# An MoE encoder block: four late expert tiles instead of two, and the expert rows loaded ahead of the last down weights

## The chip, the cores and the metric

One core of a Trainium2 chip runs the kernel. The time is the device time of one execution, in microseconds (us). Engines are named PE (TensorE), DVE (VectorE), ACT (ScalarE), POOL (GpSimd) and SP (SyncE, which here only issues transfers).

## What is computed

A two-part block on x of 512 rows by 1024 columns, all in float32. The first part (a gated causal convolution beside a sparse attention, merged and projected) is not touched by the change. The second part and the end are:

```python
h = rms_norm(x, g_ffn)
# top-1 group of 4, then top-2 of the 8 experts in it; comb = their softmax weights
for e in range(32):                       # D_MODEL 1024, EXPERT_FF 256
    a, b = h @ w_gate[e], h @ w_up[e]
    out += (silu(a) * b * comb[:, e]) @ w_down[e]
x = x + out
return rms_norm(x, g_final)
```

Each of the 512 rows goes to two experts, so there are 1024 (row, choice) products to make. The weights of an expert are 3 MB, those of all 32 are 96 MB.

## The kernel before, in words

`build` writes one program for each engine, with waits on semaphores between them. In the expert part the 32 experts are worked on in 16 pairs. A tile is 32 slots of each of the two experts of a pair; a pair has as many tiles as its fuller expert needs. The number of tiles is known only at run time: a table `tab` on the chip holds for each pair where its tiles start, and each engine loops over registers read from it. With the inputs here there are 30 tiles, 0 to 29. The pairs are put in an order by their size; the last pair (15) has one tile, tile 29, and pair 14 has tiles 27 and 28.

**Weights.** Three slots of on-chip memory (region 0, region 1, and `gates` with `conv_buf`) take turns. For pair n SP waits until the pair three before it has let go of each part, and issues eight copies of 0.5 MB for gate and up (`load_half`, L429) and two copies of 1 MB for down (`load_down`, L439). All go through SP's queue and are spread over 16 DMA engines. In `pair_tiles` (L1003) PE waits for them: `ld_gu` at L1012, `ld_dn` at L1034.

**One tile** (`pair_tiles`). 64 small products of gate and up (L1022) into bank 0; the transposes of the next tile's rows (`transpose_tile`, L980, L985) into banks 6 and 7; ACT takes the silu (L1376), DVE multiplies (L1803), PE transposes the result (L1031), DVE copies it (L1806); then 16 down products (L1039) into bank 2. ACT copies bank 2 to the buffer `ys` (L1383). POOL gathers the input rows of later tiles from memory (L622) and scatters the results to the table of expert rows in memory (L665, `expert_rows`), one half row per slot.

**The late tiles.** The last two tiles, 28 and 29, are not scattered: their entries of the scatter's index are set out of bounds (L1781), their places in `expert_rows` are set to zero by two scatters of zeros (L635), and their results are kept on the chip in the stack `late`, 128 slots by 1024. A weighted one-hot matrix `col_w` (rows by slots, made by DVE at L1784 to L1787, before tile 0) is transposed by PE (L1052) into `place`, and eight products (`late_rows`, L1076) bring the stack into the right rows, 128x512 each.

**The end.** After the last weights SP loads `g_final` (L486), waits until the scatters of tiles 0 to 27 have landed (L489), and loads the expert rows back, eight copies of 0.5 MB, one for each block b of 128 rows and each choice c (L493). For c=0, and for block 3's c=1, DVE adds the weighted rows (`add_row`, L1815); for the other c=1 rows PE makes weighted products (`weighted_row`, L1068) into the banks where `late_rows` adds its own. DVE adds each bank to x (`add_late`, L1823), ACT takes the squares (L1397), DVE the mean (L1415), POOL the power -1/2 (L671), DVE scales (`scale_out`, L1829), and SP stores (L497, L502).

The order of all this is written out by hand; each engine's program is in order. What sets the order of the transfers is SP's program:

```python
                sp.wait_ge(S["y_mm"], used)
                load_down(slot, pair)            # L482, the last of the weights
            ...
            for n in range(RING):
                sp.wait_ge(scattered[n], ((early + (RING - 1 - n)) // RING) * 16)
            sp.wait_ge(zeroed, 32)
            for b in range(TB):                  # L491
                for c in range(2):
                    sp.dma_start(y_row(b, c), ...)
```

`early` is the number of tiles that are scattered, 28 here.

Of the kernel before, what the change touches and what calls it, by code (L numbers as in the profile page):

```python
# [21 lines left out]
I32 = mybir.dt.int32  # L22
U32 = mybir.dt.uint32
# [43 lines left out]
def build(nc, x, g_mix, w_in, conv_w, conv_b, conv_ln_g, conv_ln_b, w_conv_out, w_attn_out, w_out,  # L67
# [17 lines left out]
    MAXT = 48  # L85
    assert PAIRS + (2 * T - PAIRS) // SLOTS < MAXT
# [13 lines left out]
    with ExitStack() as ctx:  # L100
# [116 lines left out]
        def piece(words):  # L217
# [32 lines left out]
        place = gluf[:, cut[0] - 256:cut[0] + 256]  # L250
        no_rows = gluf[:, 0:BANK]
        diag = gluf[:, BANK:BANK + 3 * P].rearrange("p (b n) -> p b n", b=TB - 1)
        col_code = mask[:, P:2 * P]
        col_hit = gluf[:, BANK:2 * BANK].rearrange("p (b n) -> p b n", b=TB)
        col_w = mask[:, 2 * P:6 * P].rearrange("p (b n) -> p b n", b=TB)
        first_hit = kTf[:, BANK:BANK + 2 * TB * SLOTS].rearrange("p (b e n) -> p b e n", b=TB, e=2)
        late = r1[:, 8192 + D:8192 + 2 * D].rearrange("p (n f) -> p n f", n=2)
        late_si = sb("late_si", [P, 2], U32)
# [5 lines left out]
        gidx = sb("gidx", [P, MAXT + RING + 1], U32)  # L264
        carrier = sb("carrier", [P, 6])
# [33 lines left out]
            hidT_mm hidT_ev y_mm yev_a xg_mm xtev_a xtev_v idx_copy y_add hits_ready first_mm diagw_ready late_ev col_ready late_ready place_mm place_ev late_mm late_add o_ready dve_chain pool_chain  # L299
# [66 lines left out]
        late_banks = (3, 4, 0, 1, 5, 6, 7, 2)  # L366
# [9 lines left out]
        def _(sp):  # L376
# [94 lines left out]
            sp.wait_ge(S["order_ready"], 1)  # L471
            for n in range(SETS, PAIRS):
# [11 lines left out]
            early = sp.value_load(tab[0:1, PAIRS + 1:PAIRS + 2], min_val=PAIRS - 2, max_val=MAXT - 3)  # L484
            sp.wait_ge(S["y_mm"], sp.value_load(tab[0:1, PAIRS - 2:PAIRS - 1], min_val=1, max_val=MAXT))
            sp.dma_start(g_final_bc, g_final.rearrange("(a n) -> a n", a=1).to_broadcast([P, D])).then_inc(ld_gbc, 16)  # L486
            for n in range(RING):

                sp.wait_ge(scattered[n], ((early + (RING - 1 - n)) // RING) * 16)  # L489
            sp.wait_ge(zeroed, 32)  # L490
            for b in range(TB):  # L491
                for c in range(2):
                    sp.dma_start(y_row(b, c), y_dram[c * T + b * P:c * T + (b + 1) * P, :])\  # L493
                        .then_inc(ld_y[b][c], 16)
# [3 lines left out]
            for n in range(RING):  # L498
                sp.wait_ge(scattered[n], ((early + 2 + (RING - 1 - n)) // RING) * 16)
# [1385 lines left out]
```

## Time and profile before

| | |
|---|---|
| time, median of 3 executions | 661.61 us (659.83 to 662.32) |
| the profiled execution's own time | 662.68 us |
| its span | 660.6 us |
| mean granted clock of PE | 0.966 of full |
| PE busy | 581.6 us, 88% |
| DVE, ACT, POOL busy | 345.2, 257.1, 294.8 us |
| read from memory, written | 145.11 MB, 12.60 MB |
| SP's copies (queue q1) | 139.90 MB, 57.0% of 16 engines' span |

The span is from the first to the last instruction; the execution's own time is 2.1 us longer. The expert loop starts at 390.75 us, the last down product ends at 633.4. A busy share over the whole span says little here, as stages with different limits follow on each other. "PEclk" is the clock that PE was granted: 1.0 is 2.4 GHz and 0.5 is 1.2 GHz. "SPq" is SP's queue: the time that it takes to issue transfers.

### The profile page before, as it was taken

The numbers are of one execution on the slowest core, as the hardware profiler recorded it, in microseconds if no ns is written. First come the engines' busy times: TensorE is split into PE (matmuls) and PEld (weight loads), VectorE is DVE, ScalarE is ACT, GpSimd is POOL, SyncE is SP. The second block draws the span as 40 slices with busy tenths as digits, with TensorE's granted clock in tenths as the row PEclk, the third lists the DMA queues.
The fourth block names the chain that finished last, engine by engine and source line by source line (L and its number), as shares of the span: only waits on it lengthen the run. The fifth ranks groups of instructions, "written<-read, shape, count | busy, mean of one in ns | idle before, by whom it ended". The sixth has DMA issues, their size and how long they took to land.

```text
span 660.6 us, 12497 instructions
## 1 busy us (share of the span) xinstructions
PE 581.6 (88%) x4387; PEld 384.8 (58%) x4388; DVE 345.2 (52%) x855; ACT 257.1 (39%) x444; POOL 294.8 (45%) x466
## 2 busy tenths in 40 slices
PE   3899999999999999999999876973899899988883
PEld 2577788877665676877888632432444444444431
DVE  4518999999979996169322583110111211211156
ACT  6435333244755674364413103331133333334212
POOL 5333344469996322346550016443245445544331
PEclk9999999999999999799999796998899999999987
DMA  9122632622222024031249999999997999999863
GB/s 296 46 88 65 224 95 66 137 63 65 64 65 64 0 89 168 0 128 52 108 168 357 376 406 350 408 406 408 409 405 292 409 410 407 409 406 402 350 242 127
DMA packets 64609, 149.09 MB, mean 226 GB/s; under 512 B 14372, under 2 KB 30756, under 8 KB 64574
## 3 DMA queue, kind: packets, MB, share of 16 engines
q1 hardware_dynamic: 59150, 139.90, 57.0%
q0 software_dynamic: 5280, 8.22, 3.4%
q10 hardware_dynamic: 144, 0.52, 0.2%
q8 instruction: 20, 0.33, 0.2%
q14 instruction: 15, 0.12, 0.1%
HBM read 145.11 MB, written 12.60 MB: 239 GB/s over the span
## 4 chain that ended last, share of the span: by engine, by line
PE 51%; DVE 21%; SPq 11%; DMA 9%; issue 4%; ACT 3%; POOL 1%; DVEq 0%; POOLq 0%; ACTq 0%
PE bank L704 27%; SPq L429 8%; PE bank L1022 7%; PE bank L1039 5%; DVE bm L1477 5%; DVE m L1476 4%; DMA conv_buf<-in_w_e_down 3%; DMA region<-in_w_e_up 3%; DVE conv_buf L1468 3%; SPq L439 2%; PE bank L782 2%; DMA region<-expert_rows 2%; PE bank L815 2%; PE bank L803 1%; PE bank L985 1%
## 5 line engine op out<-in xcount | busy, mean ns | idle before, releaser
L704 PE MATMUL bank<-h_hi,w_part 128*128 128x512 f32 (+1 forms) x528 | 173.4, 398 | 3.2 <-DVE h_lo L1426 1.7
L557 POOL TENSOR_TENSOR w_part<-region,w_part 128x1024 fp32r<-128x1024 f32 (+1 forms) x52 | 109.8, 2112 | 147.6 <-ACT w_part L1113 147.6
L704 PEld LDWEIGHTS bank<-h_hi,w_part 128*128 128x128 f32 (+1 forms) x528 | 98.0, 186 | 30.3 <-issue 6.8
L704 PE MATMUL bank<-h_lo,w_part 128*128 128x512 f32 (+1 forms) x264 | 102.9, 390 | 0.0
L1803 DVE TENSOR_TENSOR mask_b<-mask_b,bank 128x128 f32<-128x128 f32 x30 | 8.7, 289 | 176.8 <-ACT mask_b L1376 176.8
L1022 PE MATMUL bank<-region,kT 128*32 128x256 f32 x1408 | 82.5, 387 | 14.4 <-DMA region<-in_w_e_up 11.5
L1113 ACT ACTIVATE w_part<-region 128x1024 fp32r<-128x1024 f32 (+1 forms) x52 | 48.0, 925 | 108.0 <-PE bank L704 107.9
L607 POOL TENSOR_TENSOR carrier<-mhalf 128x1 f32<-128x1 f32 x183 | 33.3, 199 | 115.2 <-ACT qT L1383 97.5
L1022 PEld LDWEIGHTS bank<-region,kT 128*32 128x32 f32 x1408 | 50.3, 112 | 53.0 <-issue 31.4
L1511 DVE SCALAR_TENSOR_TENSOR bank<-glu,cv,bank 128x256 f32<-128x256 f32 x196 | 78.6, 479 | 0.0
L704 PEld LDWEIGHTS bank<-h_lo,w_part 128*128 128x128 f32 (+1 forms) x264 | 49.1, 186 | 9.6
L1039 PE MATMUL bank<-region,mask_b 128*32 128x512 f32 x352 | 44.0, 619 | 9.9 <-DVE mask_b L1806 9.9
L1383 ACT ACTIVATE qT<-bank 128x512 f32 x28 | 16.7, 597 | 80.6 <-PE bank L1039 80.6
L622 POOL DMA_INDIRECT bm<-h_rows,gi x34 | 36.5, 1074 | 5.0 <-issue 0.2
L665 POOL DMA_INDIRECT expert_rows<-qT,si x30 | 30.7, 1023 | 13.2 <-issue 13.1
L1376 ACT ACT_TABLE_LOAD x28 | 35.9, 1283 | 0.5
L1376 ACT ACTIVATE mask_b<-bank 128x128 f32<-128x128 f32 x30 | 8.3, 278 | 67.0 <-PE bank L1022 67.0
L1022 PE MATMUL bank<-gates,kT 128*32 128x256 f32 x512 | 29.2, 380 | 5.6 <-DMA gates<-in_w_e_up 5.1
L985 PE MATMUL bank<-ident,v_rows 128*128 128x128 f32 x124 | 23.5, 313 | 7.6 <-DVE v_rows L1798 6.8
L1022 PEld LDWEIGHTS bank<-gates,kT 128*32 128x32 f32 x512 | 18.4, 110 | 19.3 <-issue 11.8
L985 PEld LDWEIGHTS bank<-ident,v_rows 128*128 128x128 f32 x124 | 17.4, 209 | 20.9 <-issue 13.6
L565 POOL TENSOR_SCALAR bm<-glu,cv 128x512 f32<-128x512 f32 x17 | 26.6, 1565 | 0.9
(289 smaller groups left out, 909.3 us busy)
## 6 DMA issues: line engine op xcount, KB each, us to landing
region<-in_w_e_down SPq DMA_DIRECT2D x22, 1024.0 KB, 15.9
region<-in_w_e_gate SPq DMA_DIRECT2D x44, 512.0 KB
region<-in_w_e_up SPq DMA_DIRECT2D x44, 512.0 KB
region<-in_w_in SPq DMA_DIRECT2D x16, 1024.0 KB, 6.1
conv_buf<-in_w_e_down SPq DMA_DIRECT2D x10, 1024.0 KB, 18.5
gates<-in_w_e_gate SPq DMA_DIRECT2D x20, 512.0 KB
gates<-in_w_e_up SPq DMA_DIRECT2D x20, 512.0 KB
region<-in_w_out SPq DMA_DIRECT2D x2, 2048.0 KB, 7.8
```

The source lines that it names most:

```text
L429: sp.dma_start(w_gu[slot][:, e, m, half, :, :], w[0, bass.ds(pair * 2 + e, 1), rows, :].rearrange("a (p k) f -> p (a k) f", k=KD // 2))\
L557: g.tensor_tensor(unit_part(u, 1), unit_raw(u), unit_part(u, 0).bitcast(F32), ALU.subtract)\
L607: ins = g.tensor_tensor(carrier[:, n:n + 1], mhalf[:], mhalf[:], ALU.add)
L622: g.indirect_dma_start(out=ring[:, u, :], out_offset=None, in_=h2_halves, in_offset=bass.IndirectOffsetOnAxis(ap=gi1[:, u:u + 1], axis=0), ...
L704: last = mm(out_, a_parts[p], b_parts[q], start=start and x_ == 0, stop=stop and x_ == 2)
L985: last = tr(bank[6 + k // 2][:, k % 2 * P:(k % 2 + 1) * P], view[:, k, :], ident[:])
L1022: last = mm(bank[0][32 * c:32 * c + 32, 0:FF], xTs[:, k, at_:at_ + 32], w_gu[slot][:, e, :, half, k, j * P:(j + 1) * P], start=(half == 0 ...
L1039: last = mm(bank[2][32 * c:32 * c + 32, :], hidT[:, at_:at_ + 32], w_dn[slot][:, e, j, n * BANK:(n + 1) * BANK], start=(j == 0), stop=(j = ...
L1113: a(unit_part(u, 0), unit_raw(u), ACT.Copy).then_inc(S["w_hi"], 1)
L1376: a(sil, bank[0][:, 0:P], ACT.Silu).then_inc(S["silu_g"], 1)
L1477: link(v.match_replace(work[:, 0:n], m8[:], src[:, 0:n], NEG))
L1511: ins = v.scalar_tensor_tensor(out_, shifted, cv[:, c, j:j + 1], so_far, ALU.mult, ALU.add)
```

## The change

The constant `LATE = 4` takes the place of the two late tiles: tiles 26 to 29 are held back, as two stacks of two tiles, `late[0]` (26, 27) and `late[1]` (28, 29), with two `col_w` and two `place`. Four scatters of zeros stand ahead of the loop instead of two. SP issues the copies of the expert rows (`load_rows`) inside the loop over pairs, for the last pair, after its gate and up weights and before its down weights; they wait only for tiles 0 to 25. DVE makes `col_w` after tile 3 and after tile 5 instead of before tile 0. PE transposes the placements before pair 12. The eight products of stack 0 are made inside tile 29: three before its gate products, three before its hidden copy is waited for, one before its down products, one among the products of stack 1, which follow on the down products. Of the rows with c=1 only block 3's are weighted by PE, all others are added by DVE, three of them ahead of the last tile's hidden product and four behind it. ACT copies both halves of each late tile (before, DVE took one half of tile 29), and takes the squares of block 3 in two halves. If the last pair had more than one tile, the products would be made in each of them (`again`); here it is zero.

```diff
+    LATE = 4
-        late_banks = (3, 4, 0, 1, 5, 6, 7, 2)
+        late_banks = (3, 4, 5, 6, 7, 0, 1, 2)
@@ SP
+            def load_rows():
+                sp.wait_ge(S["y_mm"], sp.value_load(tab[0:1, PAIRS - 2:PAIRS - 1], min_val=1, max_val=MAXT))
+                for n in range(RING):
+                    sp.wait_ge(scattered[n], ((early + (RING - 1 - n)) // RING) * 16)
+                sp.wait_ge(zeroed, 16 * LATE)
+                for b in range(TB):
+                    for c in range(2):
+                        sp.dma_start(y_row(b, c), y_dram[c * T + b * P:c * T + (b + 1) * P, :])\
+                            .then_inc(ld_y[b][c], 16)
...
                 load_half(slot, pair, 1)
+                if n == PAIRS - 1:
+                    load_rows()
                 sp.wait_ge(S["y_mm"], used)
                 load_down(slot, pair)
-            sp.wait_ge(S["y_mm"], sp.value_load(tab[0:1, PAIRS - 2:PAIRS - 1], min_val=1, max_val=MAXT))
             sp.dma_start(g_final_bc, ...).then_inc(ld_gbc, 16)
-            for n in range(RING):
-                sp.wait_ge(scattered[n], ((early + (RING - 1 - n)) // RING) * 16)
-            sp.wait_ge(zeroed, 32)
-            for b in range(TB):
...
@@ POOL
-            for u in range(2):
+            for u in range(LATE):
                 g.indirect_dma_start(out=y_halves, ...)
@@ PE, pair_tiles
                 with pe.Fori(first, end) as t:
+                    if last_pair:
+                        pe.wait_ge(S["place_ev"], 2)
+                        pe.wait_ge(S["yev_a"], pe.value_load(rows_upto[0:1, bass.ds(t, 1)], min_val=1, max_val=MAXT))
+                        for k in range(3):
+                            late_rows(0, k)
                     pe.wait_ge(ld_gu[slot], 128 * turn + 128)
...
                     tr(bank[1][:, 0:P], hid, ident[:]).then_inc(S["hidT_mm"], 1)
+                    if last_pair:
+                        pe.wait_ge(S["xtev_a"], t + 2)
+                        pe.wait_ge(S["xtev_v"], t + 2)
+                        for k in range(3, 6):
+                            late_rows(0, k)
                     pe.wait_ge(S["hidT_ev"], t + 2)
                     pe.wait_ge(S["yev_a"], t + 1)
+                    if last_pair:
+                        late_rows(0, 6)
                     pe.wait_ge(ld_dn[slot], 32 * turn + 32)
...
                     last.then_inc(S["y_mm"], 1)
+                    if last_pair:
+                        pe.wait_ge(S["diagw_ready"], 1)
+                        pe.wait_ge(ld_y[TB - 1][1], 16)
+                        weighted_half(0)
+                        half_done = pe.value_load(half_upto[0:1, bass.ds(t, 1)], min_val=1, max_val=LATE)
+                        for k in range(2 * TB):
+                            if k == 0:
+                                pe.wait_ge(S["late_half"], half_done)
+                            elif k == 1:
+                                pe.wait_ge(S["yev_a"], t + 2)
+                            late_rows(1, k)
+                            if k == 3:
+                                late_rows(0, 2 * TB - 1)
+                                weighted_half(1)
@@ ACT
-            for u in range(2):
+            for u in range(LATE):
+                if u < 2:
+                    act.wait_ge(S["place_mm"], u + 1)
+                    a(place[u], bank[5 - u][:], ACT.Copy).then_inc(S["place_ev"], 1)
                 hidden_gate(early + u)
-                for n in range(2 - u):
+                for n in range(2):
                     for e in range(2):
...
+                    if n == 0:
+                        last.then_inc(S["late_half"], 1)
@@ DVE
-            with dve.Fori(0, early + 1) as t:
+            for t in range(6):
+                next_rows(t)
+                hidden(t)
+                if t in (3, 5):
+                    late_columns((t - 3) // 2)
+            with dve.Fori(6, early + LATE - 1) as t:
                 next_rows(t)
                 hidden(t)
...
+            rows_in = [(b, c) for b in range(TB) for c in range(2)][:-1]
+            next_rows(early + LATE - 1)
+            for b, c in rows_in[0:3]:
+                add_row(b, c)
+            hidden(early + LATE - 1)
+            for b, c in rows_in[3:]:
+                add_row(b, c)
+            for k in range(4):
+                add_late(k)
             mean_square(2, 0)
+            add_late(4)
             dve.wait_ge(ld_gbc, 32)
             scale_out(0, whole)
+            add_late(5)
             mean_square(2, 1)
+            add_late(6)
+            add_late(7)
             scale_out(1, whole)
             mean_square(2, 2)
             scale_out(2, whole)
```

## Rows read from the trace of the kernel before

**Rows 1.** The page: mean busy share of the DMA engines in 40 equal slices, tenths.

```profile
DMA  9122632622222024031249999999997999999863
```

**Rows 2.** Chain of waits in order of time, from 540 us: start, us, what.

```profile
618.53 6.08 DMA expert_rows<-qT,si
...
625.01 10.21 DMA region<-expert_rows
```

**Rows 3.** Timeline of SP's queue: start, us of issuing, engine, line, operation, tiles, count.

```profile
610.68 4.07 SPq L439 DMA_DIRECT2D region<-in_w_e_down  x2
...
624.63 3.74 SPq L493 DMA_DIRECT2D region<-expert_rows  x8
```

**Rows 4.** L439's and L493's transfers: down copies issued from 610 to 616; row copies.

```profile
L439 SPq DMA_DIRECT2D region<-in_w_e_down x2: 1506/1988/2471, 610.7 to 612.3; - x2
...
DMA to landing us min/median/max: 11.4/15.2/19.0
...
DMA to landing us min/median/max: 9.3/12.2/14.8
```

**Rows 5.** Windows of 2 us: length, PE, PEld, DVE, ACT, POOL busy, PEclk, DMA share, GB/s.

```profile
624.00:626.00 2.00, 0.41 (x4) 0.17 (x2) 0.00 (x0) 1.97 (x4) 0.00 (x0) 1.00 0.55 182
...
636.00:638.00 2.00, 2.00 (x4) 0.83 (x3) 1.91 (x2) 0.00 (x0) 0.48 (x1) 0.50 0.48 187
638.00:640.00 2.00, 2.00 (x4) 0.76 (x3) 0.03 (x1) 0.00 (x0) 0.00 (x0) 0.67 0.18 68
640.00:642.00 2.00, 2.00 (x6) 0.91 (x5) 1.90 (x3) 0.52 (x1) 0.00 (x0) 1.00 0.06 25
```

**Rows 6.** Timeline of PE: down product of tile 0; placement; last tile.

```profile
403.59 3.64 PE L1039 MATMUL bank<-region,mask_b 128*32 128x512 f32 x16 [0.38 <-DVE mask_b L1806]
...
623.75 0.66 PE L1052 MATMUL bank<-ident,mask 128*128 128x128 f32 x4
626.40 3.66 PE L1022 MATMUL bank<-region,kT 128*32 128x256 f32 x64 [1.99 <-DMA region<-in_w_e_up]
631.49 1.92 PE L1039 MATMUL bank<-region,mask_b 128*32 128x512 f32 x16 [0.38 <-DVE mask_b L1806]
```

**Rows 7.** Windows of 4 us around PE's long wait for weights, columns as in rows 5.

```profile
460.00:464.00 4.00, 0.00 (x0) 0.00 (x0) 0.00 (x0) 0.00 (x0) 0.00 (x0) 0.50 1.03 409
464.00:468.00 4.00, 3.71 (x36) 2.03 (x40) 0.00 (x0) 0.00 (x0) 0.00 (x0) 0.50 1.03 410
```

**Rows 8.** Timeline of the end, all engines.

```profile
623.88 2.39 ACT L1393 ACTIVATE region<-bank 32x512 f32<-32x512 f32 x4 [2.64 <-PE bank L1039]
...
633.91 1.28 DVE L1815 SCALAR_TENSOR_TENSOR x_rows<-region,wts,x_rows 128x1024 f32<-128x1024 f32 x1 [2.48 <-DMA region<-expert_rows]
...
640.56 1.88 PE L1068 MATMUL bank<-region,glu 128*128 128x512 f32 x4
...
642.28 1.88 PE L1076 MATMUL bank<-region,glu 128*128 128x512 f32 x4
...
650.89 1.28 DVE L1823 TENSOR_TENSOR x_rows<-x_rows,bank 128x512 f32<-128x512 f32 x2
...
652.21 1.06 ACT L1397 ACTIVATE conv_buf<-x_rows 128x1024 f32<-128x1024 f32 x1 [1.24 <-DVE x_rows L1823]
...
654.32 0.54 POOL L671 TENSOR_TENSOR rs<-ss,mhalf 128x1 f32<-128x1 f32 x1 [1.46 <-DVE ss L1415]
...
654.90 1.41 DVE L1829 SCALAR_TENSOR_TENSOR x_rows<-x_rows,rs,region 128x512 f32<-128x512 f32 x2 [0.66 <-POOL rs L671]
```

**Rows 9.** Timeline of the start of the expert loop.

```profile
399.05 0.69 DVE L1787 TENSOR_TENSOR mask<-mask,glu 128x512 f32<-128x512 f32 x1
...
400.73 0.45 DVE L1798 COPY v_rows<-bm 128x512 f32 x1 [0.99 <-POOL carrier L607]
...
402.73 0.48 PE L1031 MATMUL bank<-ident,mask_b 128*128 128x128 f32 x1 [0.36 <-DVE mask_b L1803]
...
404.17 1.03 POOL L635 DMA_INDIRECT expert_rows<-glu,late_si  x1 [0.16 <-issue]
```

More of the change, by code:

```diff
@@ L498, in _ @@
             for n in range(RING):
[L499 removed]
+                sp.wait_ge(scattered[n], ((early + LATE + (RING - 1 - n)) // RING) * 16)
             for n in range(2):
@@ L1001, in table_products, with late_rows, weighted_half, pair_tiles @@
                 last.then_inc(S["tab_mm"], 1)
-            def pair_tiles(n, slot, turn):
+            def late_rows(stack, k):
+                b, n = late_turns[k]
+                last = mm(bank[late_banks[k]][:], place[stack][:, b * P:(b + 1) * P], late[stack][:, n, :],
+                          start=(stack == 0), stop=(stack == 1))
+                if stack:
+                    last.then_inc(S["late_mm"], 1)
+            def weighted_half(n):
+                mm(bank[late_banks[2 * TB - 2 + n]][:], diag, y_row(TB - 1, 1)[:, n * BANK:(n + 1) * BANK],
+                   start=False, stop=False)
+            def pair_tiles(n, slot, turn, last_pair=False):
                 first = pe.value_load(tab[0:1, n:n + 1] if isinstance(n, int) else tab[0:1, bass.ds(n, 1)],
@@ L1046, in _ @@
                 pair_tiles(slot, slot, 0)
[L1047 removed]
+            with pe.Fori(1, PAIRS // SETS - 1) as i:
                 for slot in range(SETS):
                     pair_tiles(SETS * i + slot, slot, i)
[L1050 to L1088 removed]
+            pe.wait_ge(S["col_ready"], 2)
+            for stack in range(2):
+                for b in range(TB):
+                    last = tr(bank[5 - stack][:, b * P:(b + 1) * P], col_w[stack][:, b, :], ident[:])
+                last.then_inc(S["place_mm"], 1)
+            early = pe.value_load(tab[0:1, PAIRS + 1:PAIRS + 2], min_val=PAIRS - LATE, max_val=MAXT - 1 - LATE)
+            for n in range((PAIRS // SETS - 1) * SETS, PAIRS):
+                pair_tiles(n, n % SETS, n // SETS, n == PAIRS - 1)
         @block.scalar
@@ L1366, in _ @@
             act.wait_ge(S["tab_ready"], 1)
-            early = act.value_load(tab[0:1, PAIRS + 1:PAIRS + 2], min_val=PAIRS - 2, max_val=MAXT - 3)
-            act.wait_ge(S["col_ready"], 1)
-            for b in range(TB - 1):
-                last = a(diag[:, b, :], ident[:], ACT.Copy, scale=wts[:, 1, b:b + 1])
-            last.then_inc(S["diagw_ready"], 1)
+            early = act.value_load(tab[0:1, PAIRS + 1:PAIRS + 2], min_val=PAIRS - LATE, max_val=MAXT - 1 - LATE)
             def hidden_gate(t):
```

133 lines of the change are left out of this document (49 added, 84 removed).

## The prediction

> **What bounds the kernel now.** I read the page's slices first: the DMA engines are full in nearly every slice of the last 40% of the span [rows 1]. Then the chain of waits in order of time: before the end it passes through a scatter's landing (6.08 us) and the landing of the expert rows (10.21 us) [rows 2]. The queue of SyncE shows the order behind that: the last pair's down weights are issued at 610.68, the eight row copies only at 624.63, when the scatter of tile 27 has landed [rows 3]. The landings tell how deep the queue is: the second down copy, issued at 612.3, lands 19.0 us later, at 631.3; the last row copy, issued at 627.9 (the eighth of eight within 3.74 us), lands 14.8 us later, at 642.7 [rows 4]. The two-microsecond windows show that the engines don't end together. At 624 to 626 their mean share is 0.55 and at 636 to 638 it is 0.48, but the last data come after 640, at a share of 0.06, which is one engine of 16 [rows 5]. So one engine is some 5 us behind the bulk of them, and a copy has landed only when that one has done its part. That late engine sees no hole at 624 to 626: down weights until 631.3, then the final gain (0.5 MB), then eight rows of 0.5 MB until 642.7, which is (642.7 - 631.3) / 9 = 1.27 us for 0.5 MB, its full pace.
>
> PE meanwhile starts tile 29 (the last; its pair has only this one) at 626.40, held by its gate and up weights, and its down product at 631.49, ends at 633.41 [rows 6]. From there to the end of the span, 660.6, are 27.2 us: row adds, late rows, norm, store.
>
> **The change part by part.**
>
> *1. Rows ahead of the last down weights.* The eight row copies now stand in SyncE's queue before the two down copies. On an engine the queue is served in order in every row here, so the down weights land 8 x 1.27 = 10.2 us later on the late engine: 631.3 + 10.2 = 641.5. The bulk of the engines finish the rows at about 637 now (share 0.48 in 636 to 638 [rows 5]); without the hole (some 1.8 us) and with the final gain behind instead of ahead (1.3) they would be through with everything at about 634. I take the late engine, since PE waits for all 16; the bulk value is the other bound. The Trainium skill (DMA: Bandwidth & Descriptors, "Queues, rings and completion order") says that each engine consumes its descriptors in ring order and that a copy is complete only when all of its engines have finished; this speaks against the change, and the landing rows agree.
>
> SyncE's new waits in front of the rows are for tile 26's down product, the scatters up to tile 25 and the zeroing. Behind them stand the down copies and the final gain; PE waits for the first. Tile 26 ends before tile 27's product begins and SyncE comes to this point at 610.68 [rows 3], so I cost the waits at 0 to 1 us, take 0, and the cover is the queue's backlog of some 15 us. The hole in the bulk's work (0.45 of 2 us in 624 to 626, and a similar one before) is filled, but the late engine gains nothing from that. The final gain moves behind the down weights, 641.5 + 1.3 = 642.8, and is wanted only at the first scaling, after 650: nothing.
>
> *2. PE before the last down product.* Three first-stack products ahead of tile 29 cost 3 x 0.86 (two products lie 1.72 apart, from 640.56 to 642.28 [rows 8]) = 2.6 us. They fit between 624.4 and PE's old start at 626.40 but for about 0.6 to 1 us. Gate and up 3.66, transposes and hidden about 1.5, then four more products, 3.4: PE is ready at about 635.8. Against 641.5 all of this is free; against the bulk's landing it would be the bound. Placement is transposed for both stacks, eight instead of four at 0.66 us a group [rows 6], before pair 12 instead of after pair 14: 1.3 to 2.2 us with the issue gap. PE waits for DMA at tile 27 anyway, so at most 1 us comes through and is then covered by the late landing: 0.
>
> *3. The clock.* PE will stand idle from 635.8 to 641.5, over 5 us. When it stood idle up to 464 the granted clock was 0.50 at 460 to 464 and still 0.50 at 464 to 468 [rows 7]: 1.2 GHz. The down product at this level took 3.64 us at 403.59, against 1.92 at 631.49 [rows 6]. I take 3.64: the product ends at 641.5 + 0.1 + 3.64 = 645.2. The other bound is 1.92. The Trainium skill (TensorE: Matmul & The Clock Gate, "The HAM clock gate") calls the halved clock the default that activity lifts; with it the product costs 1.7 us more than a reading by the last tile of the trace, and rows 7 agree.
>
> *4. The tail behind that product.* Time counted from its end, E. ScalarE copies the first half of the stack: 2 x 0.60 (four took 2.39 [rows 8]), done at E+1.35. The second half is done at E+2.55. PE meanwhile makes one weighted half. Then come products 0 at E+1.4 and 1 at E+2.6, and to the end of product 3 it is E+5.2. The held-back first-stack product and the second weighted half take two more (E+6.9), products 4 to 7 four more: E+10.4. DVE adds each at 0.64 (two took 1.28). Add 4 starts at E+7.9. From there DVE is the bound: add 4 0.64, scaling 1.28, add 5 0.64, adds 6 and 7 1.28, scaling 1.28, small operations 0.25, then 0.75 waiting for POOL's power, scaling 1.28, two linked small operations 0.4, POOL 0.54 + 0.1, two half scalings 1.41: E+17.8. The squares of the last block are done in halves by ScalarE before E+13.2 (half of 1.06 each, an estimate), hidden. From DVE's last scaling (656.31) to the end are 4.3 us in the trace. Sum: 22.1 us, against 27.2 now, so 5.1 us are gained. What goes: five row adds of 1.28 and two products' worth of waiting for rows. I put this sum at 21 to 23.
>
> *5. The start.* Five column operations of 0.7 us (the last at 399.05) and ScalarE's wait for them leave the way to tile 0 [rows 9]. But DVE's row copy at 400.73 waits for the first gather, and stays; only ScalarE's late silu goes, and the transpose of the hidden rows can follow the row transposes at about 402.4 instead of 402.73. That is 0.35 us, carried on by the full DMA queue. The columns, 3.5 us, go into DVE's idle time in tiles 3 and 5, where a tile lasts 7 us and DVE waits over 5 of it: 0; with this cover gone it would be 3.5 each. Two more zeroing scatters on POOL, 1.03 and a gap each, some 2.6 us, delay tile 1's rows to about 410.3, just when PE wants them (tile 1's gate products end near 410.4): 0, at worst 0.5. Their bytes are saved again at the scatters of tiles 26 and 27, which now write nothing. ScalarE's four quarter copies (2.39 instead of 0.60) in tiles 26 and 27 end before PE's next down product: 0. Unrolled loops on PE and DVE: code is loaded in the shade of a PE that waits for DMA, 0; the trace doesn't show their cost, and I allow -0.5 to 1.5.
>
> **Sum.** 641.5 + 0.1 + 3.64 + 22.1 - 0.35 = 667.0 us of span against 660.6: +6.4. The profiled execution's own time was 662.68, 2.1 over its span and 1.1 over the median of 661.61. 661.6 + 6.4 = 668.0.
>
> **The rivals.** (A) *The lag of one engine does not show in the changed kernel*, or the down weights' last part doesn't suffer it. They land at about 634, PE's own 635.8 is the bound, the clock stays full: 635.9 + 1.92 + 22.1 - 0.35 = 659.6, one less than now, no measurable change (about 660.6 on the median). For it: the mean share at 638 to 640 is only 0.18 [rows 5], so most engines really are early. Against: the last landings of both groups of copies [rows 4], each waited for by the engine that came next. (B) *Faster*: the same early landing, and the late products fit into the tile. PE waits in each tile for the silu, the row copies and the hidden copy; if three of the seven hide there, the down product starts at 633.2 rather than 635.9 and the span is 656.9, on the median 657.9 (-0.6%). It decides at a landing of 636.8: a down product at full clock that starts later is no gain (636.8 + 0.1 + 1.92 + 22.1 - 0.35 = 660.6). (C) *Slower still*: the waits in front of the rows bite or late products run at half clock beyond the down product, 2 to 3 us on top: about 671.
>
> **How the numbers follow.** About 0.5% is what a measurement of this kernel can tell from no change, 3.3 us. My forecast has 0.62, C 0.12, A 0.17, B 0.09. For 8 in 10 the range runs from the lower edge of the forecast's case with part of A, 660.0, to 671.0. Faster 0.09; same 0.18 (A and the low edge of the forecast); slower 0.73.
>
> **What would show it.** In the changed profile: the rows' issues directly behind the last up weights, near 611, and the down copies near 620 to 624; the DMA share full through 636 with no hole at 624; the last down product near 641.6, with "DMA region<-in_w_e_down" as what ended PE's idle time, 5 us of it, and PEclk at 0.5; row adds done before it; 22 us from its end to the span's. I am wrong if the down product starts before 637, if its clock is full, or if the tail behind it is under 21 us.

## The result, and the profile after

| | before | after |
|---|---|---|
| time, median | 661.97 us (659.83 to 662.73, 4 executions) | 669.61 us (667.56 to 671.22, 4 executions) |
| span of the profiled execution | 660.6 us | 667.0 us |
| expert loop starts | 390.75 us | 391.69 us |
| PE busy | 581.6 us, 88% | 589.9 us, 88% |
| mean granted clock | 0.966 | 0.964 |

The change makes the kernel slower: the ratio is 1.0125, with a 95% interval of [1.01, 1.015], 7.6 us by the medians and 6.4 us by the profiled spans. The loop starts 0.9 us later in this execution. Over the seven profiled executions of kernels with the kernel before's tiles (before, e2, e5, e6, e9, e10, e12) its start lies between 389.0 and 391.4 us, 390.3 in the mean; over the seven with four late tiles (after, e1, e3, e4, e7, e8, e11) between 390.8 and 392.7, 391.8 in the mean. The two ranges overlap, and whether the 1.5 us between the means belong to the change is not shown. So below the span is also given from the loop's start (the first gate product): 269.9 us before, 275.3 after. What is lost ahead of the loop is not in it; it is in the ratios.

The page of after, the mean busy share of the DMA engines in 40 equal slices; it answers to [rows 1]:

```profile
DMA  9122722522222033033069999999998999999913
```

The queue of SyncE after, to be set beside [rows 3] (start, us of issuing, line, operation, tiles, count; L486 loads the rows, L443 the down weights, L502 the final gain):

```profile
610.59 1.16 SPq L433 DMA_DIRECT2D region<-in_w_e_up  x1
612.93 9.20 SPq L486 DMA_DIRECT2D region<-expert_rows  x8
622.24 3.45 SPq L443 DMA_DIRECT2D region<-in_w_e_down  x2
625.74 0.48 SPq L502 DMA_DIRECT2D region<-in_g_final  x1
```

The rows follow the last up weights after 1.2 us, so their new waits held SP for little. They take 9.20 us to issue where they took 3.74; it fits with this that in e2 below, whose queue had run nearly dry, they take 4.79, so I read the 9.20 as the pace of a full queue. The down weights leave 11.6 us later than before.

The chain of waits, in order of time, answers to [rows 2]. The scatter and the row copies are gone from it, and one piece stands in their place:

```profile
623.35 18.27 DMA region<-in_w_e_down
641.67 2.71 PE bank L1073 x16
```

The timeline of PE, for [rows 6] (L1015 is `late_rows`, two records to a product; L1049 gate and up, L1073 down, L1022 the weighted half rows):

```profile
625.92 2.84 PE L1015 MATMUL bank<-glu 128*128 128x512 f32 x6 [0.61 <-issue]
628.68 3.66 PE L1049 MATMUL bank<-region,kT 128*32 128x256 f32 x64
...
633.63 3.67 PE L1015 MATMUL bank<-glu 128*128 128x512 f32 x8 [0.18 <-issue]
641.67 2.69 PE L1073 MATMUL bank<-region,mask_b 128*32 128x512 f32 x16 [4.36 <-DMA region<-in_w_e_down]
644.28 2.02 PE L1022 MATMUL bank<-region,mask 128*128 128x512 f32 x2
646.13 3.60 PE L1015 MATMUL bank<-region,glu 128*128 128x512 f32 x8
```

Everything that could be done ahead of the last down product is done at 637.3, and PE then stands until 641.67. Before, the same product began at 631.49. The windows of 2 us (columns as in [rows 5]):

```profile
634.00:636.00 2.00, 2.00 (x6) 0.91 (x5) 1.97 (x2) 0.00 (x0) 1.01 (x1) 1.00 0.48 185
636.00:638.00 2.00, 1.30 (x4) 0.23 (x2) 1.93 (x3) 0.00 (x0) 0.00 (x0) 1.00 0.32 123
638.00:640.00 2.00, 0.00 (x0) 0.00 (x0) 0.93 (x1) 0.00 (x0) 0.00 (x0) 1.00 0.21 84
640.00:642.00 2.00, 0.33 (x4) 0.16 (x8) 0.00 (x0) 0.00 (x0) 0.00 (x0) 1.00 0.09 35
642.00:644.00 2.00, 2.00 (x16) 0.26 (x8) 0.00 (x0) 0.00 (x0) 0.00 (x0) 0.67 0.01 4
644.00:646.00 2.00, 2.00 (x6) 0.79 (x3) 0.00 (x0) 1.56 (x3) 0.00 (x0) 0.50 0.00 0
```

Two things are to be seen. The DMA share falls to 0.48 at 634 and to 0.09 at 640, though the down weights have landed only at 641.6, and PE waits for them from 637.3 on. A share of 0.09 is 1.4 engines of 16: a few engines carry the rest. And the clock is still 1.00 while PE stands; it falls only when the product has begun. The row adds, DVE's, all lie before the product, as intended (L1851; the first add of a bank, L1859, follows at 647.19):

```profile
627.72 3.97 DVE L1851 SCALAR_TENSOR_TENSOR x_rows<-region,wts,x_rows 128x1024 f32<-128x1024 f32 x3 [2.75 <-DMA region<-expert_rows]
...
633.69 5.24 DVE L1851 SCALAR_TENSOR_TENSOR x_rows<-region,wts,x_rows 128x1024 f32<-128x1024 f32 x4
```

From the product's end at 644.36 to the end of the span are 22.6 us, against 27.2 before. So the change buys 4.55 us at the end and pays for them with a product that ends 10.95 us later (644.36 against 633.41): 6.4 us more.

### The profile page after: what moved, and what is told of

The parts are those of the page before. It is cut to its first block, busy times and chain, and to the rows that moved or that the text cites. A ratio compares the mean times of both kernels' runs of the same rounds, so it can differ in the third digit from the quotient of the medians.

```text
span 667.0 us, 12502 instructions
## 1 busy us (share of the span) xinstructions
PE 589.9 (88%) x4395; PEld 387.2 (58%) x4400; DVE 350.1 (52%) x866; ACT 258.7 (39%) x451; POOL 299.8 (45%) x468
## 4 chain that ended last, share of the span: by engine, by line
PE 56%; DVE 17%; SPq 9%; DMA 7%; issue 5%; ACT 3%; POOL 1%; another core or an unknown queue 0%; POOLq 0%; DVEq 0%; ACTq 0%
PE bank L713 26%; PE bank L1049 10%; PE bank L1073 6%; SPq L433 6%; DVE bm L1499 5%; DVE m L1498 4%; DMA region<-in_w_e_down 3%; DVE conv_buf L1490 3%; PE bank L791 2%; DMA region<-in_w_e_up 2%; PE bank L994 2%; SPq L443 2%; PE bank L824 2%; PE bank L812 1%; SPq L486 1%
## 5 line engine op out<-in xcount | busy, mean ns | idle before, releaser
L1049 PE MATMUL bank<-region,kT 128*32 128x256 f32 x1408 | 83.4, 386 | 9.0 <-DMA region<-in_w_e_up 6.5
L616 POOL TENSOR_TENSOR carrier<-mhalf 128x1 f32<-128x1 f32 x183 | 34.9, 208 | 120.1 <-ACT qT L1396 89.7
L1049 PEld LDWEIGHTS bank<-region,kT 128*32 128x32 f32 x1408 | 50.2, 112 | 48.5 <-issue 26.6
L1073 PE MATMUL bank<-region,mask_b 128*32 128x512 f32 x352 | 44.8, 628 | 13.9 <-DVE mask_b L1837 8.7
L1049 PE MATMUL bank<-gates,kT 128*32 128x256 f32 x512 | 31.7, 403 | 6.8 <-DMA gates<-in_w_e_up 5.9
L1049 PEld LDWEIGHTS bank<-gates,kT 128*32 128x32 f32 x512 | 19.1, 116 | 22.3 <-issue 15.4
L994 PE MATMUL bank<-ident,v_rows 128*128 128x128 f32 x124 | 23.5, 313 | 6.2 <-DVE v_rows L1829 5.3
L1073 PEld LDWEIGHTS bank<-region,mask_b 128*32 128x32 f32 x352 | 9.6, 111 | 32.6 <-issue 24.2
```

Of the source, the lines that this page charges most:

```text
L616: ins = g.tensor_tensor(carrier[:, n:n + 1], mhalf[:], mhalf[:], ALU.add)
L994: last = tr(bank[6 + k // 2][:, k % 2 * P:(k % 2 + 1) * P], view[:, k, :], ident[:])
L1049: last = mm(bank[0][32 * c:32 * c + 32, 0:FF], xTs[:, k, at_:at_ + 32], w_gu[slot][:, e, :, half, k, j * P:(j + 1) * P], start=(half == 0 ...
L1073: last = mm(bank[2][32 * c:32 * c + 32, :], hidT[:, at_:at_ + 32], w_dn[slot][:, e, j, n * BANK:(n + 1) * BANK], start=(j == 0), stop=(j = ...
```

## The experiments

Twelve runs follow; e11 is the changed kernel again and e12 is e9 again. The figures of each, with the kernel before timed beside it on the same chip:

| kernel | ratio to before, 95% | span from the loop's start |
|---|---|---|
| before | | 269.9 |
| after | 1.0125 [1.01, 1.015] | 275.3 |
| e1, rows behind | 1.0135 [1.0084, 1.0186] | 276.7 |
| e2, order alone | 1.018 [1.0129, 1.0231] | 281.7 |
| e3, three ahead | 1.0038 [1.0014, 1.0062] | 273.0 |
| e4, kept busy | 1.0079 [1.0055, 1.0103] | 276.3 |
| e5, gain last | 0.9963 [0.9937, 0.999] | 267.4 |
| e6, ScalarE copies | 1.0 [0.9973, 1.0027] | 268.1 |
| e7, adds behind | 1.0054 [1.0022, 1.0086] | 272.4 |
| e8, last row late | 1.0017 [0.9987, 1.0047] | 270.0 |
| e9, gain before last row | 0.9982 [0.9956, 1.0008] | 266.7 |
| e10, last row on PE | 1.0009 [0.9986, 1.0031] | 267.9 |
| e11, after again | 1.0136 [1.0091, 1.0182] | 276.9 |
| e12, e9 again | 0.9961 [0.9941, 0.9981] | 267.8 |

The last column is of one profiled execution each; after and e11, or e9 and e12, are the same kernel and differ by 1.6 and 1.1 us in it. The profiled executions of e3 and e4 were moreover the slowest of their kernels, some 4 us above the medians (667.42 against 663.45, 670.72 against 666.45). So a difference of 2 us in this column is the least that says something by itself, and for e3 and e4 the ratio is the better figure.

### Is it the order of the transfers?

**e1, the changed kernel with the rows issued behind the down weights.**

```diff
-                if n == PAIRS - 1:
-                    load_rows()
                 sp.wait_ge(S["y_mm"], used)
                 load_down(slot, pair)
+                if n == PAIRS - 1:
+                    load_rows()
```

> The changed kernel with one edit: the eight row copies are issued behind the two last down copies again. Theory 1 (the copies of one DMA engine are served in order and the last engine decides, so the rows ahead cost 10.2 us of landing): the last down weights land near 631.4 instead of 641.6. The three row adds that stand before the last hidden product then become the wait: the third row lands at 631.3 + 3 x 1.27 = 635.1, the hidden product comes near 636.5, the last down product starts near 640.3 and ends near 642.3 at full clock, and with the 22.6 us behind it that the changed kernel showed the span is about 665, 2 us less than with the rows ahead. Rival (the other edits cost the 7.6 us: four zeroings, eight transposes, the products inside the last tile): down product and span stay where they are, span 667.

The time did not move. PE's timeline says why:

```profile
628.09 3.66 PE L1049 MATMUL bank<-region,kT 128*32 128x256 f32 x64
631.68 0.75 PE L994 MATMUL bank<-ident,v_rows 128*128 128x128 f32 x4
636.86 0.48 PE L1058 MATMUL bank<-ident,mask_b 128*128 128x128 f32 x1 [4.43 <-DVE mask_b L1834]
637.28 6.32 PE L1015 MATMUL bank<-glu 128*128 128x512 f32 x8
643.53 1.92 PE L1073 MATMUL bank<-region,mask_b 128*32 128x512 f32 x16
```

The wait for the down weights is gone; L1073 starts without one. But three row adds stand ahead of the last tile's hidden product in DVE's program. The first row is now late (the first add at 632.28), so the hidden product comes at 636.52, and PE waits 4.43 us for that. Here the clock fell while PE still stood, and the four stack products run at half clock, 6.32 us where they took 3.67:

```profile
634.00:636.00 2.00, 0.00 (x0) 0.00 (x0) 1.96 (x2) 0.00 (x0) 0.00 (x0) 0.95 0.39 152
636.00:638.00 2.00, 1.14 (x2) 0.69 (x3) 1.73 (x5) 0.00 (x0) 0.00 (x0) 0.50 0.32 127
```

The change moved the rows in two places, SP's queue and DVE's program, and undoing one of them leaves the other waiting.

**e7, e1 with all seven row adds behind the hidden product.**

```diff
-            for b, c in rows_in[0:3]:
-                add_row(b, c)
             hidden(early + LATE - 1)
-            for b, c in rows_in[3:]:
+            for b, c in rows_in:
                 add_row(b, c)
```

> As e1 (changed kernel, rows behind the down weights), and in addition all seven row adds stand behind the last tile's hidden product. In e1 three of them stood ahead of it: PE waited 4.43 us for the hidden product, its clock fell to half and four products took 6.32 us instead of 3.67. Theory: without them the hidden product comes at about 632.5, four products end near 636.5, the down product at 638.4 at full clock; then the first weighted half waits for the last row (641): from there 22 us as in the changed kernel with full clock, span 663, 5 us less than e1. Rival (the four zeroings, transposes and stack products cost the time by themselves): stays at 668.

The down product starts at 638.60 at full clock; the span is 4.9 us shorter than e1's. What it still waits for is the last row, for which the weighted half stands in front of the late products:

```profile
638.60 1.92 PE L1073 MATMUL bank<-region,mask_b 128*32 128x512 f32 x16
641.82 1.10 PE L1022 MATMUL bank<-region,mask 128*128 128x512 f32 x2 [1.30 <-DMA region<-expert_rows]
```

**e8, e7 with both weighted halves after the fourth late product.**

```diff
                     if last_pair:
-                        pe.wait_ge(ld_y[TB - 1][1], 16)
-                        weighted_half(0)
...
                                 late_rows(0, 2 * TB - 1)
+                                pe.wait_ge(ld_y[TB - 1][1], 16)
+                                weighted_half(0)
                                 weighted_half(1)
```

> As e7, and the two weighted halves of the last row are made behind the fourth late product, so that PE doesn't wait for the last row right behind the down product. The down product ends at 638.4 as in e7; the late adds wait only for DVE's row adds (until about 641.5) and the rest runs as in the changed kernel: span 660.5 to 661.5, level with the kernel before. Rival: the end is paced by DVE's row adds, which wait for landings, and nothing is gained over e7 (663).

```profile
637.71 1.92 PE L1073 MATMUL bank<-region,mask_b 128*32 128x512 f32 x16
640.94 4.05 PE L1015 MATMUL bank<-region,glu 128*128 128x512 f32 x8 [1.30 <-ACT region L1409]
```

That wait is gone too, and the kernel is level with the one before: 1.0017 [0.9987, 1.0047], and 270.0 against 269.9 us from the loop's start. So no loss that can be measured is left when the down weights come first and nobody waits for a row in front of the last down product and the first late products; the interval still allows 0.5%, and e8's loop started late. What it does not show is a gain: the four late tiles, their two stacks and the products inside the last tile are, in this order, worth nothing that these runs could tell from zero. Its span was expected at 660.5 to 661.5 and came out at 662.3; its loop started 1.6 us later than before's (392.35 against 390.75).

**e2, the kernel before with the rows ahead of the down weights, and nothing else.** Its edit is the same move of SP's copies, with two late tiles, so that SP must wait for the scatters up to tile 27.

> The kernel before with one edit: the row copies (still waiting for the scatter of tile 27) and the final gain in the order of the changed kernel, rows, down, gain. Theory 1: the late engine gets 8 x 1.27 us of rows between its last up weights (626.2) and the down weights; they land at 641.5, the last down product ends near 644.3, the old tail behind it shortens from 27.2 to about 23.5 since the rows lie there already: span 667 to 669, device time 669 to 671, all of the loss of the change or a little more. Rival (the order is harmless, the other edits cost the time): span 661 to 662.

It is the slowest of all, 11.8 us over before from the loop's start. The windows show a second cost beside the order (columns as in [rows 5]):

```profile
622.00:624.00 2.00, 1.59 (x16) 0.51 (x8) 0.00 (x0) 0.92 (x2) 0.00 (x0) 1.00 0.07 27
...
632.00:634.00 2.00, 0.00 (x0) 0.00 (x0) 0.00 (x0) 0.00 (x0) 0.00 (x0) 1.00 1.04 414
634.00:636.00 2.00, 0.00 (x0) 0.00 (x0) 0.00 (x0) 0.00 (x0) 0.00 (x0) 0.62 1.02 412
...
640.00:642.00 2.00, 0.00 (x0) 0.00 (x0) 0.00 (x0) 0.00 (x0) 0.00 (x0) 0.50 1.03 412
```

```profile
642.68 3.64 PE L1043 MATMUL bank<-region,mask_b 128*32 128x512 f32 x16 [12.87 <-DMA region<-in_w_e_down]
```

SP issued nothing between 609.4 and 623.63, and the queue ran nearly dry: a share of 0.07 at 622. Then rows and down weights, 6 MB, took until 642.6 at a full share. In the changed kernel the queue stays full there, since it waits for no scatter after tile 25. It also has a shorter end, 22.6 us behind the down product against 24.4 in e2. Together the rest of the change gives back 281.7 - 275.3 = 6.4 us of the 11.8 that the order costs alone.

**e3, the changed kernel with three rows ahead of the down weights and five behind.**

```diff
-                    load_rows()
+                    load_rows(slice(0, 3))
                 sp.wait_ge(S["y_mm"], used)
                 load_down(slot, pair)
+                if n == PAIRS - 1:
+                    load_rows(slice(3, 8))
```

> The changed kernel with three of the eight row copies ahead of the down copies (those that the last tile's hidden product waits for) and five behind. Theory 1: the down weights land at 626.2 + 3 x 1.27 + 5.0 = 635.1, before PE is ready for them at 637.3, the clock stays full, the last down product ends at 639.3; then PE waits for the last row (641.5) with its first weighted half, and from there it is as in the changed kernel: span about 663.3, device time 665. Rival (the rest of the change costs the time): as the changed kernel, 667 and 669. Rival 2 (the wait for the down weights is mean bandwidth, not one late engine): down weights at 631, span the same 663.

Most of the loss is gone (1.0038), and PE waits for the down weights no more. The late row takes over, as in e7:

```profile
639.98 1.92 PE L1074 MATMUL bank<-region,mask_b 128*32 128x512 f32 x16
644.77 1.10 PE L1023 MATMUL bank<-region,mask 128*128 128x512 f32 x2 [2.87 <-DMA region<-expert_rows]
```

Five rows fewer ahead of the down weights turn 5.4 us over before into 3.1 by the column, 7.6 into 2.4 by the medians, and PE has the down weights before it wants them. The wait that is left in front of the late products is for the last row; e7 and e8 show what it costs.

### How much of it is the clock?

**e4, the changed kernel with five overwritten products between the stack products and the wait for the down weights**, so that PE does not stand idle. They are 4.46 us of extra work, written into the bank that the down product overwrites.

```diff
                         late_rows(0, 6)
+                        for _ in range(5):
+                            mm(bank[2][:], place[0][:, 0:P], late[0][:, 0, :], start=True, stop=True)
                     pe.wait_ge(ld_dn[slot], 32 * turn + 32)
```

> The changed kernel with five more products of 128x512 (their result is overwritten by the down products) in the hole before the last down product, so that PE is idle under 0.5 us instead of 4.4. In the changed kernel the clock fell to 0.50 only after the product had begun, which took 2.69 us, and the weighted half after it 2.0. If the idle stretch caused that fall: down product 1.92 and weighted half about 1.1 at full clock, landing unchanged at 641.6, span 1.0 to 1.2 us less (666). If the clock falls for another reason: 2.69 and 2.0 stay. In neither case does this undo the loss.

**e11, the changed kernel once more.**

> The changed kernel once more, unaltered, beside the others on the same chip. If the first comparison holds, 1.0 to 1.5% over the kernel before (668 to 671 with the kernel before at 661), and above the one with the five overwritten products (e4), for which 1.0079 was measured, by the 0.8 us that its clock saved: the ratio would be about 1.009 to 1.013. Rival: e4's smaller ratio was only another chip; then this one also shows 1.007 to 1.008.

PE's timeline of e4, then of e11:

```profile
639.51 4.46 PE L1069 MATMUL bank<-glu 128*128 128x512 f32 x10
644.35 1.92 PE L1075 MATMUL bank<-region,mask_b 128*32 128x512 f32 x16 [0.39 <-DMA region<-in_w_e_down]
646.21 1.12 PE L1022 MATMUL bank<-region,mask 128*128 128x512 f32 x2
```

```profile
642.10 3.48 PE L1073 MATMUL bank<-region,mask_b 128*32 128x512 f32 x16 [4.80 <-DMA region<-in_w_e_down]
645.50 1.23 PE L1022 MATMUL bank<-region,mask 128*128 128x512 f32 x2
```

Kept busy, the product takes 1.92 us, where it takes 2.69 in one execution of the changed kernel and 3.48 in another. From its start to the end of the span are 24.55 us in e4, 25.3 in after and 26.1 in e11. So the clock costs 0.8 to 1.6 us of what follows on the landing, and undoing that leaves most of the loss, as expected. The other part of the expectation missed: the landing was to stay at 641.6 and the span to come out at 666, but in the profiled execution the down weights landed at about 644.3 and the span was 668.9. With its loop 0.9 us later than after's, 1.8 us of this later landing are not explained. By the ratios e4 is 0.6% better than e11, more than these 1.6 us (0.24%) give; their intervals meet between 1.0091 and 1.0103, and what is beyond 1.6 us is not explained here.

### Is there a gain in the order of the kernel before?

The final gain stands ahead of the rows there, though its 0.5 MB are first used by the first scaling, at 644.7, and the first row is waited for at 633.9.

**e5, the kernel before with the gain behind the rows.**

```diff
-            sp.dma_start(g_final_bc, ...).then_inc(ld_gbc, 16)
             for n in range(RING):
...
                         .then_inc(ld_y[b][c], 16)
+            sp.dma_start(g_final_bc, ...).then_inc(ld_gbc, 16)
```

> The kernel before with one edit: the final gain (0.5 MB) is loaded behind the eight row copies instead of ahead of them. Theory 1 (a queue served in order, the end paced by its landings): every row copy lands 1.3 to 1.6 us earlier, the gain at 642.8, before its first use at 644.7. The first row add moves from 633.9 to about 632.5 and PE's first weighted rows from 635.4 to about 634; DVE is the bound from 640 on, so 1 to 1.5 us less: 660. Rival (the end is DVE's work, not the landings): 661 as before.

Faster, 0.9963 [0.9937, 0.999]. In before PE waited 1.95 us for its first row, and the clock was at 0.50 from 636 to 638 [rows 5]; in e5 it waited 0.54 us and the clock stayed full. Each is one execution. PE's timeline of before, then of e5, then DVE's of e5:

```profile
635.36 3.23 PE L1068 MATMUL bank<-region,glu 128*128 128x512 f32 x4 [1.95 <-DMA region<-expert_rows]
638.38 2.35 PE L1076 MATMUL bank<-region,glu 128*128 128x512 f32 x4
```

```profile
634.11 1.96 PE L1068 MATMUL bank<-region,glu 128*128 128x512 f32 x4 [0.54 <-DMA region<-expert_rows]
635.90 1.88 PE L1076 MATMUL bank<-region,glu 128*128 128x512 f32 x4
```

```profile
642.92 1.28 DVE L1829 SCALAR_TENSOR_TENSOR x_rows<-x_rows,rs,region 128x1024 f32<-128x1024 f32 x1 [1.29 <-DMA region<-in_g_final]
```

The last line is the new wait: the gain now comes last, at 642.8, and the first scaling stands 1.29 us for it.

**e9 and e12, e5 with the gain issued between the last two row copies.**

```diff
                 for c in range(2):
+                    if (b, c) == (TB - 1, 1):
+                        sp.dma_start(g_final_bc, ...).then_inc(ld_gbc, 16)
                     sp.dma_start(y_row(b, c), ...)
```

> The kernel before, with the final gain issued between the copies of row (3,0) and row (3,1), instead of ahead of all rows (before) or behind them (e5). My theory: every 0.5 MB copy lands 1.27 us after the one ahead of it, and what counts is which copy is the last that somebody still waits for. The gain should land at about 641.5 and the 1.29 us that the first scaling waited for it in e5 should go; the last row lands near 643 and is wanted by DVE only at about 645. Span about 657.5 against 658.8 in e5 and 660.6 before; ratio to the kernel before 0.993 to 0.996. Rival: DVE is not the bound there and the wait only moves to the last row or to the second scaling; span as in e5, 658.8, ratio 0.996 to 0.998.

> The kernel with the final gain between the last two row copies once more, since the two versions of this move measured 0.9963 [0.9937, 0.999] and 0.9982 [0.9956, 1.0008], one interval without 1 and one with it. If the 1.3 us that the late landing of the rows loses are real, the ratio is 0.996 to 0.999 and the wait of the first scaling is for POOL and not for the gain. Rival: no gain; ratio 0.9995 or more.

DVE's timeline of e12, the first scaling:

```profile
641.08 1.28 DVE L1831 SCALAR_TENSOR_TENSOR x_rows<-x_rows,rs,region 128x1024 f32<-128x1024 f32 x1 [0.57 <-POOL rs L673]
```

The wait for the gain is gone in both executions. The ratios are 0.9982 [0.9956, 1.0008] and 0.9961 [0.9941, 0.9981]. The second interval excludes 1, so a gain of some 0.2 to 0.4% over the kernel before is there, and on the same chip e9 stands at 659.62 us where the changed kernel (e11) has 669.76, 1.5% less. That it is better than e5 the times don't show.

**e6, e5 with ScalarE copying both halves of the last late tile** in place of DVE, and **e10, e6 and e9 together with the last row weighted by PE** instead of added by DVE.

> As e5, and ScalarE copies both halves of the last late tile, as the changed kernel does, in place of DVE's two copies (1.40 us on DVE, behind the first row add). The late products can start at about 636 instead of 636.6 to 638.4, and DVE is rid of 1.4 us on its critical stretch: 2.5 to 4 us less than before in all, 657 to 658.5. Rival: PE's products or the landings of the rows pace the end, and it stays at e5's time.

> The kernel before with three edits together: the gain between rows (3,0) and (3,1); ScalarE copies both halves of the last late tile; and row (3,1) is weighted by PE (four blocks of the diagonal instead of three), so that DVE makes one row add fewer. My theory: from the last down product to the first scaling DVE is the bound, so one add of 1.28 us fewer shortens the end by about that much: span 656 to 656.5, time near 657.5 to 658.5 with the kernel before at 661, ratio 0.994 to 0.997. Rival: PE, which then makes two products more (1.7 us), becomes the bound before the last adds, and nothing is won over the kernel with the gain alone: span 657.5 to 658.5, ratio 0.996 to 1.0.

Both missed: 1.0 and 1.0009. With the 1.40 us of copies taken from DVE it only waits in their place, as its next work hangs on rows; with the add taken too, the chain from add to squares, mean and power comes out in the open. DVE's timeline of e6, then of e10:

```profile
634.92 1.28 DVE L1814 SCALAR_TENSOR_TENSOR x_rows<-region,wts,x_rows 128x1024 f32<-128x1024 f32 x1 [1.44 <-DMA region<-expert_rows]
```

```profile
643.47 1.28 DVE L1831 SCALAR_TENSOR_TENSOR x_rows<-x_rows,rs,region 128x1024 f32<-128x1024 f32 x1 [1.13 <-POOL rs L673]
...
647.16 0.15 DVE L1417 TENSOR_SCALAR ss<-ss 128x1 f32<-128x1 f32 x1 [1.21 <-ACT conv_buf L1399]
```

DVE, the engine that the expectations took for the bound, was busy with work that covered these waits.

## Why the prediction was right, and where its terms were off

The forecast's case came true: slower by more than 0.5%, and for the reason given. 668.0 us was predicted and 669.61 is the median, inside the range.

**Rows ahead of the down weights** (step 1): right. The landing was put at 641.5 and came at 641.6. The late engine decides, as forecast: the mean DMA share was down to 0.48 at 634 to 636, 6 us earlier (the sign "full through 636" was some 3 us too late, the share being 0.89 at 632 to 634; step 1's own 634 for the bulk was right). e3 and e8 confirm the step from the other side: with five rows moved behind the down weights most of the loss is gone, and with all of them behind and the waits for rows moved too, nothing measurable is left. e1, the first try at this, failed by my own expectation, because I had moved the copies back and not the three adds that were placed for the early rows.

**PE before the last down product** (step 2): right in what it weighs. PE was ready at 637.3, not 635.8. The 1.5 us are the first three products: PE came to them only at 625.92, and the gate product behind them started 2.3 us later than before, where the step had 0.6 to 1 and some 8.6 us from there to the end of the stack products, as measured. All of it is covered by the wait. But the fast rival B was dead for a second reason, since its limit was 636.8.

**The clock** (step 3): the size was off. The step took the product at 3.64 us; it took 2.69, 0.95 less, because the clock was 1.00 through the 4.36 us of idle and fell after 642. In e11 it fell earlier in the product, which took 3.48, and in e2, after 12.87 us of idle, it took the full 3.64. So the bounds of 1.92 and 3.64 were right and the value between them differs from execution to execution. I had read [rows 7] and the Trainium skill (TensorE: Matmul & The Clock Gate, "The HAM clock gate"), with whose halved default e2's long idle agrees, as if the clock were already low when work comes back. The wrong sign was "PEclk at 0.5" with the end of PE's idle time: it was 1.00 there. "If its clock is full", which would have refuted the forecast, did not come true either, since the product took more than 1.92. On the other side the weighted half behind it ran at half clock, 2.02 us instead of 1.12, which the sum had left out.

**The tail** (step 4): 22.6 us against 22.1. Add 4 started 8.0 us after the product's end (7.9 predicted); the difference comes at the first scaling, which waited 0.80 us for POOL's power:

```profile
652.34 0.69 DVE L1859 TENSOR_TENSOR x_rows<-x_rows,bank 128x512 f32<-128x512 f32 x1 [1.82 <-PE bank L1015]
653.83 1.28 DVE L1865 SCALAR_TENSOR_TENSOR x_rows<-x_rows,rs,region 128x1024 f32<-128x1024 f32 x1 [0.80 <-POOL rs L680]
```

**The start** (step 5): the sum took 0.35 us, and no run shows it. The down product of tile 0 began 10.85 us after the loop, 2.0 sooner than before (12.84): the step had held the first row copy to be fixed by the gather, but the transposes behind it came 9.0 us after the loop's start instead of 10.5. But the next gate and up products gave it back:

```profile
402.54 3.64 PE L1073 MATMUL bank<-region,mask_b 128*32 128x512 f32 x16 [0.50 <-DVE mask_b L1837]
405.95 3.37 PE L1049 MATMUL bank<-region,kT 128*32 128x256 f32 x47
409.78 2.15 PE L1049 MATMUL bank<-region,kT 128*32 128x256 f32 x17 [0.46 <-issue]
...
415.62 3.66 PE L1049 MATMUL bank<-gates,kT 128*32 128x256 f32 x64 [0.36 <-issue]
```

They last from 405.95 to 411.93, 6.0 us, against 3.73 before, with an issue gap in them, and tile 2 begins 23.9 us after the loop's start, against 23.5 before. Counted from the loop's start the down weights landed at 249.9 us, and at 250.8 in e11, where the step had 641.5 - 390.75 = 250.75; 0.35 us can't be read from that. At tile 27 PE waits for the transfer of its weights anyway (0.93 us). Which of the unrolled code, the zeroing scatters or the clock makes the 2 us was not tried.

**The sum.** Landing 641.62, 0.05 to the start, 2.69, 22.64: 667.0 us. The predicted terms, 641.5, 0.1, 3.64, 22.1 and -0.35, give 667.0 too. The agreement to a tenth is luck: the clock's 0.95 too much is made up by 0.54 in the tail, 0.35 at the start and 0.1 at the landing. The loop's start, 0.9 us later in this execution, is in no term: from there the sum gives 276.2 us, where after took 275.3 and e11 276.9. By the medians the forecast was +6.4 us, and +7.6 (after) and +9.2 (e11, 669.76 against 660.53) were measured; the part over 6.4 is assigned to no step.

## What to carry to other kernels

In these runs the queue that was full to the end served its copies in order, so the place of each transfer in it is a decision like any other: put first what is waited for first, and count every 0.5 MB ahead of it at the full pace (1.27 us here). Read the landing by the last engine and not by the mean share: between a share of 0.48 and the landing lay some 6 us. And when transfers are moved, move with them, in the programs of all engines, the work that was placed for their old time; if an edit and its undoing cost the same, look for a second wait that has taken the place of the first.

## What the runs showed of the hardware that was not expected

In after and e11 the granted clock did not fall while PE stood idle for 4.4 and 4.8 us, but after the work had come back: it was 1.00 at 640 to 642 in both, and in the next two windows 0.67 and 0.50 in after, 0.58 and 0.57 in e11, under a busy PE. That is no rule for an idle of this length: in e1, with 4.43 us of it (632.4 to 636.9), the clock fell inside, being 0.95 at 634 to 636, where PE did nothing, and 0.50 in the next window. With 12.87 us (e2) it fell inside too, at 634 to 636. Shorter waits went both ways: in the kernel before 1.95 us of waiting for a row were followed by products of 3.23 and 2.35 us instead of 1.96 and 1.88, while in e3 the clock stayed at 1.00 through a wait of 2.87 us and behind it. So a wait of 2 to 5 us can cost its price before or in the work behind it, or nothing, and its length alone doesn't say which.

The lag of the late engines was gone where the queue had run nearly dry. In e2, before whose last 6 MB the share was 0.07, the mean share stays at 1.03 until 642 and is followed at once by the landing (642.6): the 16 increments of its last row copy lie between 636.1 and 637.4, within 1.3 us, where in the kernel before they lie 5.9 us apart. In after, the same data at the end of a full queue went with over 7 us of a share under 0.5. e2 is one execution; that the emptying is what brings the engines together is the likely reading, and not tried by itself.
